# The first weight tile of nine stages, with feature tiles in the outer loop and both token halves inside

## The reference

```python
x = first_block(x, ...)    # HGRN2, gated linear attention and mLSTM branches
x = second_block(x, ...)   # convolution branch, retention branch, gated mixing
return third_block(x, ...) # stick-breaking attention, SSD and RWKV-7 branches, gated mixing
```

## Time and profile before

| | |
|---|---|
| Timed runs | 5185.12 us median of 3 (5183.34 to 5194.6) |
| Profiled execution | 5192.46 us, span 5190.7 us |
| TensorE busy | 4789.1 us, 92% of the span, 22888 matmuls |
| DVE, ACT, POOL busy | 2389.7, 1191.0, 1101.7 us |
| TensorE's mean granted clock | 0.94 |

### The profile page before, as it was taken

The page is one execution under the profiler, slowest core; times in us unless marked ns, Lnnn a source line. Parts: engine busy times, 40 slices in busy tenths (PEclk is TensorE's granted clock), DMA queues, the critical chain, the costliest instruction groups (busy, mean ns, idle before and its releaser), DMA issues. The chain is left out here.

```text
span 5190.7 us, 57030 instructions
## 1 busy us (share of the span) xinstructions
PE 4789.1 (92%) x22888; PEld 3734.7 (72%) x22888; DVE 2389.7 (46%) x2459; ACT 1191.0 (23%) x1438; POOL 1101.7 (21%) x570
## 2 busy tenths in 40 slices
PE   7999888989999999988999999999999899997978
PEld 5888776768777787776777777868777556565667
DVE  6544555351312212998654315233241444446854
ACT  3332322021111112221202212121121222224412
POOL 2222113132213131000223213222131111112221
PEclk8999997799999999999999889898999999998988
DMA  3111213121212121122422102010110211116541
GB/s 112 57 55 53 78 61 118 49 81 45 65 36 71 43 63 64 59 102 83 148 69 76 39 20 66 13 54 29 38 44 19 79 57 62 61 37 218 171 162 57
DMA packets 115604, 365.27 MB, mean 70 GB/s; under 512 B 12916, under 2 KB 14468, under 8 KB 115272
## 3 DMA queue, kind: packets, MB, share of 16 engines
q1 hardware_dynamic: 83104, 297.15, 17.3%
q10 hardware_dynamic: 32296, 65.11, 3.3%
HBM read 267.62 MB, written 94.58 MB: 70 GB/s over the span
## 5 line engine op out<-in xcount | busy, mean ns | idle before, releaser
L464 POOL CAST b_w_hi<-b_w 128x1024 fp32r<-128x1024 f32 x246 | 281.9, 1146 | 3706.3 <-PE ps L544 2758.2
L544 PE MATMUL ps<-b_hi,b_w_hi 128*128 128x512 f32 x1920 | 775.6, 404 | 70.1 <-DVE b_w_lo L479 18.0
L544 PE MATMUL ps<-b_hi,b_w_lo 128*128 128x512 f32 x1920 | 753.4, 392 | 0.0
L544 PE MATMUL ps<-b_lo,b_w_hi 128*128 128x512 f32 x1920 | 752.9, 392 | 0.0
L466 POOL TENSOR_TENSOR b_w_lo<-b_w,b_w_hi 128x1024 fp32r<-128x1024 f32 x246 | 639.0, 2597 | 19.7
L544 PE MATMUL ps<-h_hT_hi,b_w_hi 128*128 128x512 f32 x1216 | 520.1, 428 | 14.9 <-PEq L95 5.1
L544 PE MATMUL ps<-h_hT_lo,b_w_hi 128*128 128x512 f32 x1216 | 489.3, 402 | 0.0
L544 PE MATMUL ps<-h_hT_hi,b_w_lo 128*128 128x512 f32 x1216 | 488.6, 402 | 0.0
L544 PEld LDWEIGHTS ps<-b_hi,b_w_hi 128*128 128x128 f32 x1920 | 363.7, 189 | 171.2 <-issue 61.6
L544 PEld LDWEIGHTS ps<-b_lo,b_w_hi 128*128 128x128 f32 x1920 | 364.1, 190 | 81.2 <-issue 9.3
L544 PEld LDWEIGHTS ps<-b_hi,b_w_lo 128*128 128x128 f32 x1920 | 363.6, 189 | 77.4
(11 more groups left out here) (624 smaller groups left out, 7719.2 us busy)
## 6 DMA issues: line engine op xcount, KB each, us to landing
b_w<-in_w SPq DMA_DIRECT2D x277, 512.0 KB, 3.7
scratch_x_park<-xT SPq DMA_DIRECT2D x24, 512.0 KB, 4.3
xT<-scratch_x_park SPq DMA_DIRECT2D x16, 512.0 KB, 6.9
scratch_gate_park<-ret_fill_out ACTq DMA_DIRECT2D x32, 256.0 KB, 2.0
scratch_o_park<-ret_o ACTq DMA_DIRECT2D x16, 512.0 KB, 4.0
scratch_gate_park<-rw_fill_out ACTq DMA_DIRECT2D x32, 256.0 KB, 2.0
scratch_sb_park<-rw_fill_out ACTq DMA_DIRECT2D x32, 256.0 KB, 2.0
scratch_xz_park<-sb_fill_out ACTq DMA_DIRECT2D x32, 256.0 KB, 2.0
```

Source lines behind the costliest of these rows:

```text
L464: pool.tensor_copy(hi, w).then_inc(self.rounded, 1)
L544: ins = pe.matmul(out[:, t], w, y, start=start, stop=stop)
```

## The change

`multiply_as_cut` is new. For a first tile it takes the same 48 matmuls with the feature tile in the outer loop and both token halves inside: one wait, then three matmuls into half 0's bank and three into half 1's. Each accumulator gets its products in the same order as before. `multiply_part` is rewritten in the same way, for all eight half-tiles of the narrow projection, those without `y_cut` too. The other eight places call `multiply_as_cut` for their first tile. The first mLSTM fill tile in block 1 (L1459) also has a `y_cut` and stays as it is.

```diff
@@ norm_and_first_tile @@
-            stream.multiply(pe, out, 0, y_cut=cut)
+            stream.multiply_as_cut(pe, out, 0, cut)
@@ multiply_part @@
-        for n, (half, ky, t, w, y, start, stop) in enumerate(self.passes(k % self.RING, halves, nk, part)):
-            if n == 0:
-                pe.wait_ge(self.cut, k + 1)
-            if y_cut is not None and half == 0 and n % 3 == 0:
+        todo = list(self.passes(k % self.RING, halves, nk, part))
+        pe.wait_ge(self.cut, k + 1)
+        for ky in range(nk):
+            if y_cut is not None:
                 pe.wait_ge(y_cut, ky + 1)
-            ins = pe.matmul(out[:, t], w, y, start=start, stop=stop)
+            for _, at, t, w, y, start, stop in todo:
+                if at == ky:
+                    ins = pe.matmul(out[:, t], w, y, start=start, stop=stop)
         ins.then_inc(self.done, 2)
@@ Stream @@
+    def multiply_as_cut(self, pe, out, k, y_cut, halves=None):
+
+
+        todo = list(self.passes(k % self.RING, halves or (self.y_hi, self.y_lo)))
+        pe.wait_ge(self.cut, k + 1)
+        for ky in range(KD):
+            if isinstance(y_cut, tuple):
+                pe.wait_ge(y_cut[ky % 2], ky // 2 + 1)
+            else:
+                pe.wait_ge(y_cut, ky + 1)
+            for half, at, t, w, y, start, stop in todo:
+                if at == ky:
+                    ins = pe.matmul(out[:, t], w, y, start=start, stop=stop)
+                    if stop:
+                        ins.then_inc(self.done, 2)
@@ stream_projection (the gated, conv and conv-norm projections likewise) @@
-                stream.multiply(pe, out[e % 2], base + e, halves=halves, y_cut=y_cut if e == 0 else None)
+                if e == 0:
+                    stream.multiply_as_cut(pe, out[0], base, y_cut, halves)
+                else:
+                    stream.multiply(pe, out[e % 2], base + e, halves=halves)
```

More of the change, by code:

```diff
@@ L2044, in _ @@
                     pe.wait_ge(added, e - 1)
-                stream.multiply(pe, pair(core, e % 2), base + e, y_cut=y_cut if e == 0 else None)
+                if e == 0:
+                    stream.multiply_as_cut(pe, pair(core, 0), base, y_cut)
+                else:
+                    stream.multiply(pe, pair(core, e % 2), base + e)
                 if e == 1:
@@ L2130, in _ @@
                     pe.wait_ge(added, e - 3)
-                stream.multiply(pe, bank(e), base + e, y_cut=y_cut if e == 0 else None)
+                if e == 0:
+                    stream.multiply_as_cut(pe, bank(0), base, y_cut)
+                else:
+                    stream.multiply(pe, bank(e), base + e)
         @block.scalar
@@ L2245, in _ @@
             for e in range(2):
-                stream.multiply(pe, pair(core, e), base + e, y_cut=y_cut if e == 0 else None)
+                if e == 0:
+                    stream.multiply_as_cut(pe, pair(core, 0), base, y_cut)
+                else:
+                    stream.multiply(pe, pair(core, e), base + e)
             for k in range(KD):
```

## The result

The changed kernel takes 5159.68 us, median of 5 executions (5155.95 to 5168.21); the kernel before, on the same chip, 5186.74 (5 executions, 5183.34 to 5195.27). The ratio is 0.9945, 95% interval 0.9931 to 0.9960: 28.5 us less by the ratio, 27.1 by the medians. On two other chips the pair gave 0.9947 (0.9935 to 0.9959) and 0.9939 (0.9927 to 0.9952).

A forecast was written before the change was run, and what follows sets the result against it. TensorE is busy 92% of the span, so time goes only where it waits or runs at lower clock. Terms summed to 24.0 us, taken off the median 5185.12: 5161.1, own range 5153 to 5170, widened to 5152 to 5177.

The forecast's parts named there:

- Norm stages: Three norm stages: first tile ends 4.9 us earlier, but POOL's cut of weight tile 1 limits the gain; sum 8.8 us.
- Conv-norm projection: First tile: 42 matmuls done before the last low half, arriving unchanged, then six; gain 6.8 us, 5.5 if cold.
- Conv projection: First tile: cold for 4.0 us as before, then full pace, 12.9 us against 14.12; gain 1.3 us, felt by ACT's next rounding.
- Gated projection: First tile: twelve matmuls done by the third arrival, clock then most likely risen; gain 3.6 us, 1.4 if it rises later.
- Plain projection of block 2: First tile: 42 matmuls without a stall after the second arrival, clock rising after 5.5 us; gain 2.4 us, bounds 0.9 and 3.4.
- Plain projection of block 3: First tile: as in block 2, at 0.233 us per matmul, ending at 5083.9; gain 2.3 us, bounds 0.9 and 3.4.
- Narrow projection: First half-tile: half-clock pace already fills the gaps; gain 0.2 us, bounds 0 and 0.5; seven other half-tiles 0.
- Behind the norms: After norm stages: TensorE idles 2.0 us for POOL and its clock may drop; loss 1.4 us, bounds 0 and 3.6.
- Changes of accumulator: All changed tiles: 160 more changes between two accumulators cost 0; upper bound 0.13 us each, 21 us.
- the rival in which half is eaten: Whole kernel: clock drops after norms, late clock rises and DVE's centring leave 13.4 us, time 5172; chance 12%.
- DVE's centring: Conv-norm stage, part of a rival: DVE's centring holds the stage for half its gain, 3.4 us.
- the prediction's own signs of being wrong: Profile after: pauses at half changes, a stage end unmoved, low-half arrivals moving, half clock in tiles after norms 2 and 3.

The follow-up runs named there:

- norms alone: Only the three norm stages put in the new order, against the kernel before; 5173.99 us, ratio 0.9970.
- idle matmuls: Nine matmuls with unread results added behind each norm stage's first tile, against the changed kernel; 5154.80 us, on another chip 5160.29 us.

## Why the prediction was right, point by point

*Norm stages: 8.8 predicted, 8.7 in the profile, 11.3 by the means.* The last matmul starts at 48.12 (48 predicted) and the next stage at 50.52 (50.6), right behind POOL's cut. Taking that cut from POOL gave 1.8 us more per stage, so the limit was named rightly. What the sum missed is that the profile of before happened to hold three of the shorter stages; that 8.8 met 8.7 so closely in the first pair of profiles is luck.

*Conv-norm projection: 6.8 predicted, 5.4.* All the steps came but one: the prediction had said that the arrivals stay where they are and that no DMA moves within a stretch, and the arrival of the last low half did move.

```profile
2469.42 1.23 DVE L2308 TENSOR_TENSOR b_lo<-cnorm_stage,b_hi 128x1024 fp32r<-128x1024 f32 x1 [3.38 <-ACT b_hi L2291]
...
2470.70 0.50 PE L544 MATMUL ps<-b_hi,b_w_hi 128*128 128x512 f32 x1 [2.95 <-DVE b_lo L2308]
...
2472.56 1.04 POOL L464 CAST b_w_hi<-b_w 128x1024 fp32r<-128x1024 f32 x1 [24.86 <-PE ps L544]
```

It started at 2469.42, not 2468.11, since its input came later from DRAM. With the order of the kernel before it starts 25.5 us into the stage (25.54, 25.50 and, norms alone, 25.46). With the new order it lies anywhere from 25.2 to 27.5 in eleven profiles, and POOL's next cut starts 3.1 to 3.6 us behind that. So the tile now ends with its last input, and the gain at POOL is 4.8 to 7.2 us (35.5 less 30.7 or 28.3) according to that transfer. The six matmuls behind it ran at full clock (0.34 and 0.23 us apart), which the term had assumed; in three of the eleven profiles the clock fell right behind them and took 1.2 to 1.6 us of the gain again. Why the transfer varies more than it did isn't settled; no run took its neighbours on the queue away.

*Conv projection: 1.3 predicted, 0.2.* The step that failed is "cold for 4.0 us, which doesn't change". In this profile the clock rose 6.1 us after the first matmul (the pace goes from 0.43 to 0.23 us at 2353.3), and the stretch's clock is 0.78 for 0.86. ACT's next weight rounding then waits as long as before:

```profile
2361.26 1.06 ACT L473 ACTIVATE b_w_hi<-b_w 128x1024 fp32r<-128x1024 f32 x1 [18.78 <-PE ps L544]
2362.35 1.23 DVE L479 TENSOR_TENSOR b_w_lo<-b_w,b_w_hi 128x1024 fp32r<-128x1024 f32 x1 [6.24 <-ACT b_w_hi L473]
```

That the moment of the rise decides it is borne out by all ten profiles with the new order: where the clock rose 3.5 to 4.4 us after the first matmul the stage took 95.35 to 95.82 us (six profiles), where it rose after 6.1 to 6.4 us, 96.66 to 96.72 (four). With the old order it took 96.92 to 96.95 in four profiles, whether the rise came after 3.0 or after 6.1 us. So the gain lies between 0.2 and 1.6, 0.9 on the mean. (The term's own working, 14.12 less 12.9, gives 1.2.)

*Gated projection: 3.6 predicted, 3.6.* DVE, which waits for the tile, starts at 2581.41 for 2590.50, with the stage's start 5.47 us earlier: 3.6 us, as in every kernel with this edit (99.32 to 99.40 us).

*Plain projection of block 2: 2.4 predicted, 3.4 at the tile and 1.5 at the stage's end.* DVE's first addition comes 16.1 us after the stage's start (2680.59 - 2664.48), where it was 19.5 (2693.09 - 2673.57). TensorE then carries that to the end of the products, and there the norm's closing sums of squares (L180, L185) run colder than before: L180 takes 4.14 us for 3.63 and L185 3.55 for 2.14, the 1.9 us that are missing at the end. At the tile the clock rose 3.6 us after the first matmul; the term had taken 5.5, and its upper bound, a rise at the second arrival, is what came. L185 alone (columns: PE busy, PEld busy, granted clock, DMA share, GB/s; block 2, then block 3; the clock is that of the whole stretch, and one is shorter), before:

```profile
2760.00:2780.00 20.00, 2.14 (x16) 2.08 (x16) 0.85 0.27 97
5160.00:5180.00 20.00, 3.55 (x16) 3.53 (x16) 0.67 0.07 27
```

and after:

```profile
2755.00:2770.00 15.00, 3.55 (x16) 3.53 (x16) 0.65 0.29 107
5130.00:5150.00 20.00, 2.46 (x16) 2.40 (x16) 0.83 0.22 88
```

*Plain projection of block 3: 2.3 predicted, 5.5.* The tile itself gave 2.6 (its clock rose after 5.0 us, not 5.5; the term's own ends, 5086.02 and 5083.9, are 2.1 apart). The other 2.9 are the same sums with the other sign: at the end of block 3 they were cold before and mostly warm after. L180 took 4.83 us before and 3.63 after, L185 3.55 and 2.46: 2.3 us. The 64 transposes of the output behind them (L683, now L701) took 10.1 and 9.2, of which 0.6 reaches the end. All fourteen profiles agree on both: the end of the kernel lasts 123.1 to 123.9 us with the old order and 118.4 to 118.6 with the new, and block 2's 102.5 to 103.7 and 101.1 to 101.4. So this belongs to the change. That it comes by way of the moment at which the last products end is the likely reading, but no run moved that moment alone; the sum had no such term. The prediction carried a tile's gain to the stage's end unchanged, and that step was wrong in size both times.

*Narrow projection: 0.2 predicted, 0.4.* In this profile the agreement is chance. DVE's first addition, which waits for the first half-tile, starts 10.66 us into the stage, for 10.57 before: the tile gave nothing. The 0.4 appear at the stage's end, where the last sums (L185) start 0.4 us earlier, once more the closing sums.

*Behind the norms: -1.4 predicted, -1.4 behind norm 1 and -4.8 in retention in this profile, -2.6 by the means.* The sum put the loss down to clock drops after the wait for POOL, and that step isn't borne out. One drop came, behind norm 2, for 1.5 us; behind norm 1 the next weight tile's matmuls start 13.6 us later and at half clock in every kernel, the old ones too. The rest of the 4.8 is a longer first unit (247.18 for 243.85) and a longer second one (233.66 for 232.2). By the means below the two stages lost 2.6 us, with a standard error of 1.0. But the five profiles in which TensorE waits for POOL have 993.18 and 1215.42 us, and the five in which it doesn't (tile 1 cut elsewhere, or idle matmuls) 993.62 and 1215.67, no less. So the sign came, and what loses the time stays open; that it is the wait for POOL isn't shown.

*Changes of accumulator: 0 predicted, 0 shown.* The rule weighed there, of the Trainium skill (TensorE: Matmul & The Clock Gate; it stands in the section on a second HAM failure mode, right behind HAM oscillation), tells of another kernel that had idle spells while cycling through banks. In this kernel the runs show no such effect: with 602 further changes two stages stayed the same to 0.02 us.

*RWKV stage: not in the sum.* Ten profiles with the norms in the new order have 1226.6 to 1252.8 us, mean 1235.7; four with the old order 1236.0 to 1244.7, mean 1240.5. The difference of 4.8 us has a standard error of 3.1, so it isn't shown. Whether norm 3's earlier end shifts the clock behind it, as the earlier end of block 3's products may do for the closing sums, stays open.

The means of all profiles put the parts together. The groups are the profiles that have a stage's edit (of the norms, and of what lies behind them, or of the projections) and those that have not; for the norm stages themselves, the new order's group leaves out the five profiles with further edits there:

| stage | old order, mean (profiles) | new order, mean (profiles) | less | predicted |
|---|---|---|---|---|
| three norms | 87.67 (4) | 76.32 (5) | 11.3 | 8.8 |
| behind norms 1 and 2 | 992.65, 1213.73 (4) | 993.40, 1215.55 (10) | -2.6 | -1.4 |
| narrow | 57.41 (4) | 57.07 (10) | 0.3 | 0.2 |
| conv | 96.94 (4) | 96.06 (10) | 0.9 | 1.3 |
| conv-norm | 127.89 (3) | 122.53 (11) | 5.4 | 6.8 |
| gated | 102.98 (4) | 99.35 (10) | 3.6 | 3.6 |
| plain, block 2 | 102.96 (4) | 101.17 (10) | 1.8 | 2.4 |
| plain, block 3, to the end | 123.67 (4) | 118.48 (10) | 5.2 | 2.3 |
| sum | | | 25.9 | 24.0 |

The three timed pairs gave ratios of 0.9945, 0.9947 and 0.9939: 28 to 32 us. RWKV's 4.8 would bring the sum to 30.7; without it 2 to 6 us are left over. For the norms alone the means give 11.3 - 2.6 = 8.7, or 13.5 with RWKV, for the timed 15.6 (10.9 to 20.8 by its interval); again what is left over is about RWKV's size.

So the main steps held: POOL's cut ends the norm stages, the next engines wait for the whole tile, and changing accumulators is free. Each term has the right sign and none is off by more than 2.9. The total is also helped by chance: conv-norm gave 1.4 less and block 2's plain stage 0.6 less, block 3's 2.9 more, by the closing sums above all; the norms gave 2.5 more, and the loss behind them was 1.2 larger and not by the step that was named. Of the rival in which half is eaten, only a loss behind the norms came, 2.6 of its 3.6 us; the gated and plain tiles kept their gains, and DVE's centring ate nothing. Of the prediction's own signs of being wrong two appeared: a low half's arrival moved (conv-norm), and half clock followed norm 2 in this profile. DVE's idle time in the conv stage was 6.24 us, not 5.2.

## What to carry to other kernels

Where an operand arrives in pieces, let each piece release all the matmuls that can use it, across accumulators; changing the accumulator costs nothing here, and the work left behind the last piece falls from 27 matmuls to six. Then look for who ends the stage next (here another engine's cut of the following weight tile, worth 1.8 us more per stage). Judge such a change by the lengths of the stages around it: a long stage elsewhere whose clock wanders by 1 or 2% hides or feigns a gain of this size.

## What the runs showed of the hardware

- The same 2.4 us wait of TensorE behind norm 2 was followed by half clock in one execution and by full clock in two others of one kernel. Over the profiles, waits of 2.3 to 2.4 us at a stage change were followed by half clock in 3 of 10 cases and pauses of 0.5 to 0.7 us in none of 18. In the conv-norm tile the clock fell behind waits of 1.9, 2.0 and 3.6 us and held behind 2.5, 2.8 and 3.0.
- One stage of 6528 matmuls took 1226.6 to 1252.8 us over the fourteen profiles, with a mean granted clock of 0.92 to 0.94 and the other engines' busy time unchanged.
- Where the granted clock falls near the end of a block is not chance alone: L185's 16 matmuls at the end of block 3 took 3.55 us in four profiles with the old order there and 2.35 to 2.46 in ten with the new one; at the end of block 2 it was the other way round (2.00 to 3.20, then 3.54 or 3.55).
- Twelve norm stages of one order fall into two groups, 28.1 to 28.6 and 30.1 to 30.8 us, by the moment at which the clock rises in them (14 to 22 us in, or 25 to 27).
- Alternating between two banks cost nothing here: 98 further changes of accumulator in a stage of 384 or 388 matmuls left its length the same to 0.02 us, with the granted clock at 0.96 to 0.97.
